# Loads of the first two tiles' attention rows, issued between the fourth and the fifth chunk of w_out

## The reference

```
h = rms_norm(x, norm_pre)
z = h @ w_in                          # columns split among all groups, the last 1024 are the gate
o_att, y_pool, y_conv = ...           # three branches, together 1024 columns wide
mixed = concatenate([o_att, y_pool, y_conv]) * silu(gate)
out = rms_norm(mixed @ w_out, norm_post)
y = x + out
```

## Time and profile before

| | us |
|---|---|
| median of three runs | 1399.71 |
| lowest and highest of the three | 1398.7 and 1400.1 |
| profiled execution, its own time | 1398.08 |
| profiled execution, its span | 1396.3 |
| output stage begins | about 996 |
| TensorE's busy share of the whole span | 92% |

### The profile page before, as it was taken

The page is one execution under the profiler, slowest core; times in us unless marked ns, Lnnn a source line. Parts: engine busy times, 40 slices in busy tenths (PEclk is TensorE's granted clock), DMA queues, the critical chain, the costliest instruction groups (busy, mean ns, idle before and its releaser), DMA issues. The chain is left out here.

```text
span 1396.3 us, 21384 instructions
## 1 busy us (share of the span) xinstructions
PE 1280.3 (92%) x7456; PEld 1054.8 (76%) x7456; DVE 834.4 (60%) x1799; ACT 625.9 (45%) x1271; POOL 485.3 (35%) x420
## 2 busy tenths in 40 slices
PE   4889989989765899999999999989779999999998
PEld 3768768677534788888988888875568888888885
DVE  3467676686674888888898888854233233332412
ACT  5424142342422677777777777744322212221211
POOL 5236136262363235234152341019513222232302
PEclk9999999999975899999999999999899999999999
DMA  7524162251517032231331321645353131323211
GB/s 238 159 88 167 41 207 72 79 176 55 186 42 132 1 103 70 79 98 40 88 86 45 101 60 39 188 124 157 108 186 121 61 121 61 121 72 110 80 60 39
DMA packets 141696, 141.71 MB, mean 101 GB/s; under 512 B 55637, under 2 KB 110902, under 8 KB 140118
## 3 DMA queue, kind: packets, MB, share of 16 engines
q1 hardware_dynamic: 133350, 112.19, 27.3%
q0 software_dynamic: 5360, 17.68, 4.3%
q10 hardware_dynamic: 2880, 10.49, 2.4%
HBM read 104.08 MB, written 46.71 MB: 108 GB/s over the span
## 5 line engine op out<-in xcount | busy, mean ns | idle before, releaser
L1291 ACT ACTIVATE pT<-tp 128x512 fp32r<-128x512 f32 (+2 forms) x320 | 168.6, 532 | 106.2 <-PE tp L1230 96.6
L1348 DVE TENSOR_SCALAR_CACHE_REDUCE prob<-sc 128x512 f32<-128x512 f32 (+2 forms) x320 | 192.9, 603 | 31.7 <-PE sc L1222 17.5
L1357 DVE TENSOR_TENSOR big<-tp,pT 128x512 fp32r<-128x512 f32 (+2 forms) x320 | 193.8, 607 | 27.4 <-ACT pT L1291 26.8
L2006 PE MATMUL m<-w_gate,q2a 128*128 128x512 f32 x768 | 179.9, 394 | 4.7 <-POOLq L1984 4.7
L1230 PE MATMUL tp<-ident,prob 128*128 128x128 f32 x1088 | 171.7, 273 | 1.1 <-DVE big L1357 1.1
L1281 ACT ACTIVATE prob<-prob,nm 128x1024 f32<-128x1024 f32 (+2 forms) x192 | 171.6, 894 | 1.2 <-DVE nm L1351 0.7
L2006 PEld LDWEIGHTS m<-w_gate,q2a 128*128 128x128 f32 x768 | 144.2, 189 | 34.2 <-POOLq L1984 4.8
L701 DVE SCALAR_TENSOR_TENSOR acc<-aT,cols,acc 128x512 f32<-128x512 f32 x232 | 163.1, 751 | 10.2 <-DVE qst L777 0.9
L2168 DVE SCALAR_TENSOR_TENSOR shared<-m,rq,g_post 128x512 f32<-128x512 f32 x32 | 22.5, 746 | 233.7 <-POOL rq L1978 233.7
L1230 PEld LDWEIGHTS tp<-ident,prob 128*128 128x128 f32 x1088 | 128.6, 141 | 25.2 <-issue 1.7
L894 PE MATMUL mm<-big,w_in 128*128 128x512 f32 x576 | 140.8, 402 | 4.8 <-ACTq L585 4.8
(11 more groups left out here) (291 smaller groups left out, 2293.2 us busy)
## 6 DMA issues: line engine op xcount, KB each, us to landing
xtok<-in_x ACTq DMA_DIRECT2D x20, 512.0 KB, 4.5
xraw<-in_xT SPq DMA_DIRECT2D x17, 512.0 KB, 4.4
QT<-qst SPq DMA_DIRECT2D x32, 256.0 KB, 3.0
LAT<-in_cache_ckv SPq DMA_DIRECT2D x128, 64.0 KB, 2.1
k2a<-Y SPq DMA_DIRECT2D x16, 512.0 KB, 5.5
shared<-in_x SPq DMA_DIRECT2D x16, 512.0 KB, 4.3
out_y<-shared SPq DMA_DIRECT2D x16, 512.0 KB, 2.9
raw<-QT SPq DMA_DIRECT2D x7, 1024.0 KB, 5.0
```

The costliest lines, as they stand in the source:

```text
L1291: act.activation(pT[0][:, 4 * c:4 * c + w // P, (t % 4) * P:(t % 4 + 1) * P], tp[n % NTP][:, 0:w].rearrange("p (k q) -> p k q", q=P), ACT. ...
L1348: dve.tensor_scalar(prob[:, slot[m % J], 0:w], sc[b][:, 0:w], -1.0, None, ALU.mult, ALU.min, accum_out=top).then_inc(sc_free[b], 1)
L1357: dve.tensor_tensor(cut(1), tp[n % NTP][:, 0:w].rearrange("p (k q) -> p k q", q=P), f32(cut(0)), ALU.subtract)\
L2006: last = pe.matmul(out, w(pw_, k), x(px, k), start=(k == 0 and q == 0), stop=(k == n - 1 and q == 2))
```

## The change

`load_y`, which issues the load of one tile's attention rows, is taken out of `tile`. For the tiles from the third on it is called at the same place as before. For the first two it is called in the loop over the chunks of w_out, at k = 4, behind the wait that chunk 4 has for its staging buffer and ahead of chunk 4's own load.

```
+                def load_y(T):
+                    n = T.rows
+                    sp.dma_start(yt[:, T.b, :, 0:n], a["Y"][:, bass.ds(T.t * P, n)].rearrange("(k p) n -> p k n", p=P)).then_inc(y_ld[T.b], 16)
+
                 def tile(T, ahead=True, back=True):
                     n = T.rows
                     if ahead:
                         load_x(T.t + 2, T.b)
                     if back:
                         sp.wait_ge(s["mixed"], T.t - 1)
-                    sp.dma_start(yt[:, T.b, :, 0:n], a["Y"][:, bass.ds(T.t * P, n)].rearrange("(k p) n -> p k n", p=P)).then_inc(y_ld[T.b], 16)
+                        load_y(T)
                     if back:
                         store(T.t - 2, P, T.b)
...
                 for k in range(MC):
                     if k >= WB:
                         sp.wait_ge(s["w_lo"], k - WB + 1)
+                    if k == MC // 2:
+                        load_y(Tile(0, 0))
+                        load_y(Tile(0, 1))
                     sp.dma_start(stage[:, k % WB, :], a["w_out"][k * P:(k + 1) * P, :]).then_inc(staged[k % WB], 16)
                 tile(Tile(0, 0), back=False)
                 tile(Tile(0, 1), back=False)
```

## The result

The changed kernel takes 1404.08 us (median of six runs, 1402.02 to 1406.81) against 1399.9 us before (six runs, 1397.41 to 1403.8). The ratio is 1.0028 with a 95% interval of 1.0015 to 1.0042, which is 2.1 to 5.9 us slower. The forecast was +3.5 us, 1403.2 us, in a range of 1400.9 to 1405.1 us. The profiled execution has a span of 1400.2 us against 1396.3 us: +3.9 us.

What follows compares the result with a forecast made beforehand. TensorE's restart after waiting on staged w_out loads and GpSimd's split was taken as the bound. Chunk delay 3.5 us, gain 0 and clock 0 summed to +3.5 us: 1403.2 us against the 1399.71 us median, range 1400.9 to 1405.1 us.

Steps and rivals of the forecast that it cites:

- What bounds the kernel: Output stage: TensorE is full from 1035 to 1370 us, so only its restart, after 7.85 us idle until 1029.88, can move.
- The gain counted at 0: Ahead of tile 0: the 0.96 us wait for attention rows goes, but GpSimd's split of x tile 2 still ends last.
- The price of the two tiles: On SP's queue: 1 MB of attention rows ahead of chunk 4 makes it land at 1019.3, a delay of 3.55 us.
- the two bounds: Chunk 4's landing: 1018.8 to 1019.2 by the moving stream's price, 1019.45 by the burst at the stage's start.
- The way through chunks 5 to 7: Loads of w_out: with chunk 5 close behind chunk 4 or far, chunk 7 lands at 1027.1, 3.5 us later.
- the close one: Chunk 5 lands 1.25 us behind chunk 4, at 1020.55; chunk 7 is issued at 1022.9 and takes 4.2 us.
- the sign that I gave myself: Chunk 7's load: the pairing is wrong if it isn't 3.3 to 4.3 us behind its issue.
- What stays: TensorE restarts 3.5 us later, at about 1033.4; low clock after the pause counted 0, with 0.4 us either side.
- The first: Rival: chunk 7 lands only 2.2 us later and subtractions gain up to 0.96 us; +1.2 to +2.8 us, chance 0.20.
- The second: Rival on SP's queue: chunk 4's issue waits until Y tile 0 has drained; +4.9 us, 1404.6 us, chance 0.12.
- The third: Rival: the tiles slip through idle queues without delaying the chunks, giving back 0.96 us; 1398.8 us, chance 0.06.
- the upper end of the sum: Chunk 4 at 1019.65, then 2.15, 2.37 and 4.2 us, puts chunk 7's landing at 1028.4, 4.8 us later.

Runs made afterwards that it cites:

- loading x tile 2 early: Kernel before, with x tile 2 and tile 0's attention rows loaded behind chunk 1 and x tile 2 cast ahead of chunk 4: ratio 0.9987 (0.9971 to 1.0002).
- six buffers: Kernel before with six staging buffers for w_out, tile 0's x rows waiting for the sixth subtraction: ratio 0.9931 (0.9905 to 0.9956), median 1388.73 us.
- x tile 2 waits: Changed kernel with x tile 2's load waiting for the last subtraction of w_out: TensorE restarts 25.50 us after the common start, 21.88 us in the changed kernel.
- four buffers: Kernel before with four staging buffers for w_out, two of them the output rows' buffers: ratio 0.9951 (0.993 to 0.9972), -6.9 us.
- four buffers, x tile 2 early: Four staging buffers, with x tile 2 and tile 0's attention rows issued behind chunk 5, against the kernel before: ratio 0.9929 (0.9906 to 0.9952), -9.9 us.
- on ScalarE's queue: Changed kernel with both attention-row loads issued by ScalarE on its own queue: TensorE restarts 2.09 us later than before, against 4.45 us in the changed kernel.

## Why the prediction was right, point by point

**What bounds the kernel** held: the body of the stage is full, and the loss is a later restart of TensorE.

**The gain counted at 0** held. The split's end plus 0.55 us released the first subtraction in both kernels, and 6.31 us stand against 6.28 us from chunk 7's cast to TensorE. Loading the rows behind chunk 1 shows that the wait alone is worth nothing, and loading x tile 2 early shows what covered it.

**The price of the two tiles** held: chunk 4 was forecast at 1019.3 and cast at 1019.37, between the two bounds (1018.8 and 1019.45). One tile cost half (1.82 us), and the same two tiles ahead of chunk 7 cost 3.55 us. Chunk 4 was issued at 1013.47, a little before the earliest time that I gave (1013.7), since the first of the two issues took 0.38 us; nothing hung on it. The estimate from the 358 GB/s that the Trainium skill gives (DMA: Bandwidth & Descriptors, section "Where 436 GB/s comes from"), 0.6 us lower, would have missed by 0.7 us; the trace decides for the dearer rows.

**The way through chunks 5 to 7** held in its form: of the two ways, the close one came (chunk 5's cast 1.24 us behind chunk 4's), and chunk 7 was issued at 1022.96, forecast 1022.9. The term that was mis-sized is chunk 7's own load, 5.03 us where I took 4.2 us from chunk 5 today. By the sign that I gave myself (3.3 to 4.3 us behind its issue) I was wrong in this pairing. Chunk 5 has nothing behind it in its queue, chunk 7 has x tile 2 right behind it; without that it took 4.5 us.

**What stays** was mis-sized the other way: I counted the clock at 0 with 0.4 us to either side, and the first 12 matmuls took 0.48 us less than before. The two errors, +0.9 and -0.5 us, make the measured +3.9 us out of the forecast +3.5 us. That they offset each other is luck: over the traces of all these kernels the same 12 matmuls took 4.34 us to 5.46 us after a pause, in no order by its length, and with 5.46 us the sum would have come to +5.0 us.

**The rivals.** The first (chunk 7 only 2.2 us later, subtractions gain) is refuted by both its halves: chunk 7's cast is 4.40 us later, and the subtractions gain nothing. The second (the queue holds chunk 4 back) isn't seen: chunk 4's issue took 1.15 us and not 0.33 us, but it landed at 1019.35, between the two bounds, and not at 1020.25. The third (the tiles slip through) fails on this queue, and ScalarE's queue shows what slipping through would have looked like for chunk 4: 0.30 us.

**The range** has two slips. Its lower end, 1400.9 us, is the bottom of the first rival (+1.2 us) and so leaves out nothing of it; and the upper end of the sum starts from chunk 4 at 1019.65, 0.2 us above the higher bound, for which I gave no row. Neither decided the outcome.

## What to carry to other kernels

A load that is brought forward stands ahead of something. Find the first load behind it on the same queue that an engine waits for; if there is no slack there, expect to pay the transfer time of what was put ahead (3.6 us for two tiles here), while the gain is at most the wait that it removes. Before a visible wait is counted as a gain, look at what else gates the next instruction: here a GpSimd instruction ended at the same time and took over the 0.96 us at once. And where a pause comes from staged loads that wait for their buffers, look for buffers that stand empty at that time before changing the order of the loads: six buffers gave 9.4 us here, the best order tried with two buffers 1.3 us, both by the traces.

## What the runs showed that I had not expected

The load of a chunk that follows another closely took longer when something else followed it in turn. With two or four staging buffers and no attention rows moving ahead of it, a chunk issued 1.1 to 1.4 us after the one ahead took 4.1 to 4.7 us with nothing right behind it (4.30 us for chunk 5 before, 4.48 us for chunk 7 in the run where x tile 2 waits), and 4.8 to 5.9 us with another load right behind it (5.03 us in the changed kernel, 5.93 us with four buffers). A chunk that was issued over 2.1 us after the one ahead didn't show this: chunk 7 took 3.32 us before, with x tile 2 issued 0.38 us behind it, and chunk 6, with nothing right behind it, 3.13 us.

Two queues don't share the engines as I assumed. With 1 MB on ScalarE's queue at the same moment, SP's chunk 4 lost 0.30 us and chunk 5, 1.1 us behind it, 2.02 us.

The cost of the low clock after a pause varies more than I had allowed. The first 12 output matmuls took 4.34 us to 5.46 us after pauses of 2.57 us to 15.91 us, with no order by length (5.42 us after 3.71 us, 4.69 us after 15.91 us), against 2.96 us at the full clock. The 48 gate matmuls at the stage's start took 12.51 us to 14.06 us in the profiled executions, although nothing in them was changed; this alone moves a profiled execution by up to 1.5 us. The granted clock accounts for the lengths: in each trace with such a pause it was at 0.50 (1.2 GHz) at the restart, and the 12 matmuls took 4.34 us where it was back at 1.00 some 2.9 us later (four buffers, x tile 2 early) and 5.46 us where that took some 5.5 us (on ScalarE's queue). What decides how soon it comes back isn't settled by these runs.
